# First tile and input block in pieces, and the first norm as row sums on ScalarE

## The reference, cut to what matters

```python
def rmsnorm(u, g):
    u32 = u.astype(jnp.float32)
    r = lax.rsqrt(jnp.mean(u32 * u32, axis=-1, keepdims=True) + NORM_EPS)
    return (u32 * r * g.astype(jnp.float32)).astype(u.dtype)
...
        h = rmsnorm(x, g[0])
...
    z = h @ w_in
    hy = dwconv3(z[..., :HY_STREAMS * D_HY], hy_short_w, hy_short_b)
```

## Time and profile before

| | before |
|---|---|
| median of three runs | 2406.3 us |
| profiled execution | 2411.59 us |
| its span, first to last instruction | 2409.7 us |
| mean granted TensorE clock | 0.993 |
| PE busy | 2368.3 us |
| DVE busy | 1327.8 us |
| ACT busy | 1096.8 us |
| DMA, mean | 185 GB/s |

### The profile page before, as it was taken

How to read it: one execution, slowest core, us unless ns; L and a number is a source line. 1 busy time by engine, 2 the same in 40 slices (tenths; PEclk the granted TensorE clock), 3 DMA queues, 4 the chain that set the end, 5 groups by cost and what they waited for, 6 DMA issues and landing times.

```text
span 2409.7 us, 25541 instructions
## 1 busy us (share of the span) xinstructions
PE 2368.3 (98%) x11089; PEld 1965.2 (82%) x11089; DVE 1327.8 (55%) x1318; ACT 1096.8 (46%) x1159; POOL 27.7 (1%) x49
## 2 busy tenths in 40 slices
PE   7999999999999999999999999999999999999998
PEld 6778787788888888888888888888888878888887
DVE  5565855544544554556764444554444576656554
ACT  5444443644443344344554444344344455544343
POOL 1000000000000000000000000000000000000000
PEclk9999999999999999999999999999999999999999
DMA  7445455555555555555455555555555545643344
GB/s 283 159 158 187 173 198 193 190 188 188 188 204 192 192 189 188 188 186 209 182 185 191 188 182 190 192 192 188 192 181 190 188 156 196 238 159 140 123 149 149
DMA packets 63103, 446.08 MB, mean 185 GB/s; under 512 B 7209, under 2 KB 7540, under 8 KB 11215
## 3 DMA queue, kind: packets, MB, share of 16 engines
q1 hardware_dynamic: 60080, 427.60, 49.8%
q0 software_dynamic: 2912, 16.85, 1.9%
HBM read 442.33 MB, written 2.10 MB: 184 GB/s over the span
## 4 chain that ended last, share of the span: by engine, by line
PE 92%; DVE 3%; DMA 2%; ACT 2%; issue 1%; POOL 0%; ACTq 0%; POOLq 0%; SPq 0%; DVEq 0%
PE P L329 89%; PE P L332 3%; DVE raw_r L596 1%; ACT hi L487 1%; DMA raw<-in_w_z 1%; DMA raw<-in_w_i 1%; DVE R_h L583 0%; DMA raw<-in_w_d 0%; DVE X L583 0%; DVE EV L639 0%; ACT R_h L483 0%; DVE R_m L580 0%; DMA raw<-in_w_u 0%; ACT EV L509 0%; DMA raw<-in_w_ukv 0%
## 5 line engine op out<-in xcount | busy, mean ns | idle before, releaser
L596 DVE TENSOR_TENSOR raw_r<-raw,hi 128x2048 fp32r<-128x2048 f32 (+3 forms) x412 | 928.3, 2256 | 955.5 <-ACT hi L487 955.1
L329 PE MATMUL P<-hi,R_h 128*128 128x512 f32 (+2 forms) x3840 | 1234.6, 396 | 17.9 <-DVE raw_r L596 10.9
L487 ACT ACTIVATE hi<-raw 128x2048 fp32r<-128x2048 f32 (+3 forms) x412 | 776.5, 1887 | 1010.8 <-DMA raw<-in_w_d 390.1
L329 PEld LDWEIGHTS P<-hi,R_h 128*128 128x128 f32 x3840 | 727.3, 190 | 170.2 <-DVE R_h L583 18.1
L329 PE MATMUL P<-hi,R_f_r 128*128 128x512 f32 x2480 | 777.3, 391 | 0.1
L329 PE MATMUL P<-raw_r,R_h 128*128 128x512 f32 (+2 forms) x1920 | 749.7, 390 | 0.0
L329 PEld LDWEIGHTS P<-hi,R_f_r 128*128 128x128 f32 x2480 | 465.6, 188 | 96.7 <-DVE raw_r L596 0.6
L329 PE MATMUL P<-raw_r,R_f_r 128*128 128x512 f32 x1240 | 482.7, 389 | 0.0
L329 PEld LDWEIGHTS P<-raw_r,R_h 128*128 128x128 f32 x1920 | 364.6, 190 | 73.7 <-issue 3.8
L329 PEld LDWEIGHTS P<-raw_r,R_f_r 128*128 128x128 f32 x1240 | 233.0, 188 | 47.1
L332 PE MATMUL P<-ident,EV 128*128 128x128 f32 (+2 forms) x486 | 72.5, 272 | 0.2 <-ACT EV L483 0.2
(11 more groups left out here) (192 smaller groups left out, 838.6 us busy)
## 6 DMA issues: line engine op xcount, KB each, us to landing
raw<-in_w_u SPq DMA_DIRECT2D x128, 1024.0 KB, 4.8
raw<-in_w_d SPq DMA_DIRECT2D x128, 1024.0 KB, 4.8
raw<-in_w_z SPq DMA_DIRECT2D x48, 1024.0 KB, 4.8
raw<-in_w_i SPq DMA_DIRECT2D x36, 1024.0 KB, 4.8
raw<-in_w_mo SPq DMA_DIRECT2D x16, 1024.0 KB, 4.8
raw<-in_w_o SPq DMA_DIRECT2D x16, 1024.0 KB, 4.7
raw<-in_w_mkv SPq DMA_DIRECT2D x8, 1024.0 KB, 4.8
R_g<-in_rows POOLq DMA_DIRECT2D x6, 1024.0 KB, 5.9
```

Source lines behind the costliest of these rows:

```text
L329: return self.e.matmul(o, l, r, start=start, stop=stop, skip_group_check=True)
L487: self.e.activation(hi, raw, ACT.Copy).then_inc(*self.inc("high_made", ("high", k, d)))
L596: self.e.tensor_tensor(low, raw, hi.bitcast(f32), ALU.subtract).then_inc(*self.inc("low_made", *names))
```

## The change

Four things are edited. First, tile 0 and the first of the four input blocks are loaded in pieces, each with a semaphore of its own, in turn: columns 0, slice 0, columns 1, slice 1, columns 2 and 3, slices 2 and 3; columns and splits of tile 0 alternate on ACT and DVE. Second, `cols` is loaded from ACT's queue, and ACT makes a first small copy (`first_table`) before the input is waited for, so that its table load stands there. Third, `X` is loaded from SP's queue behind `ident` and ahead of tile 4, in four pieces with a semaphore each; POOL's loads of the filter's tables wait for its last piece. Fourth, the first norm takes its sums from `X` with `square_sum` and the ordinary `rstd`; `first_squares` in its old form, `first_reduce` and `first_sums` are gone, and so is the wait of the bias load.

```diff
@@ -192,7 +192,6 @@
 
 
         self.XT = v3(R_g[:, :], 16)
-        self.SQ = R_m[:, :]
         self.f_emb, self.f_w1, self.f_w2 = R_s[0:33, 2048:2304], R_s[0:33, 2304:2368], R_s[0:64, 2368:2432]
         self.f_a, self.f_b = v3(R_f[:, 0:2048], 2), v3(R_f[:, 2048:4096], 2)
         self.f_win, self.f_w3 = v3(R_f[:, 4096:6144], 2), R_f[0:65, 6144:8192]
@@ -349,13 +348,6 @@
             last = self.tr(o, i)
         last.then_inc(*self.inc("turn_done", done))
 
-    def first_sums(self, b, src, ready, free, done):
-        self.wait_ge(free)
-        self.wait_ge(ready)
-        for t in range(2):
-            last = self.mm(self.m.P[b][:, t:t + 1], src[:, 128 * t:128 * t + 128], self.m.half[:, 0:1], True, True)
-        last.then_inc(*self.inc("turn_done", done))
-
     def filter_hidden(self, b, l, r, ready, free, done):
         self.wait_ge(ready)
         self.wait_ge(free)
@@ -483,7 +475,7 @@
         self.e.activation(o, i, ACT.Copy, **scale).then_inc(*self.inc("act_done", done))
 
     def split(self, k, d, hi, raw, low):
-        self.wait_ge(("loaded", k))
+        self.wait_ge(("loaded", k) if k else ("loaded", k, d))
         self.e.activation(hi, raw, ACT.Copy).then_inc(*self.inc("high_made", ("high", k, d)))
 
     def cols_ready(self, m):
@@ -498,10 +490,14 @@
         for d, g in enumerate(gains):
             self.copy(h[:, d, :], p[:, d, :], (done, "high", d), scale=g)
 
-    def first_squares(self, g, ready, done):
-        self.wait_ge(ready)
-        q = slice(1024 * g, 1024 * g + 1024)
-        self.e.activation(self.m.SQ[:, q], self.m.R_g[:, q], ACT.Square).then_inc(*self.inc("act_done", done))
+    def first_table(self, ready, done):
+
+        self.wait_ge(ready)
+        self.copy(self.m.st[:, 0:2], self.m.half[:, :], done)
+
+    def first_load(self, sem, o, i, done):
+        if sem == "c4":
+            self.e.dma_start(o, i).then_inc(*self.landed(sem, done))
 
     def square_sum(self, src, dst, o, ready, free, done, **scale):
         self.wait_ge(ready)
@@ -632,12 +628,6 @@
     def times_row(self, dst, src, row, ready, done):
         self.wait_ge(ready)
         self.tt(dst, src, row, ALU.mult, done)
-
-    def first_reduce(self, k, ready, free, done):
-        self.wait_ge(ready)
-        self.wait_ge(free)
-        self.e.tensor_reduce(self.m.EV[k][:, 0:256], self.m.SQ.rearrange("p (c t) -> p t c", c=16), AX.X, ALU.add
-                             ).then_inc(*self.inc("dve_done", done))
 
     def sine(self, z, cb, o, ready, done):
         m = self.m
@@ -920,8 +910,12 @@
         self.wait_ge(free)
         self.e.dma_start(o, i).then_inc(*self.landed(f"ring{k % NS}", ("loaded", k)))
 
+    def load_piece(self, d, o, i):
+        self.e.dma_start(o, i).then_inc(*self.landed(f"w{d}", ("loaded", 0, d)))
+
     def first_load(self, sem, o, i, done):
-        self.e.dma_start(o, i).then_inc(*self.landed(sem, done))
+        if sem != "c4":
+            self.e.dma_start(o, i).then_inc(*self.landed(sem, done))
 
     def store(self, t, q, ready, done):
         self.wait_ge(ready)
@@ -971,10 +965,7 @@
         while not listing and not at_["pause"] and at_["high"] < min(at_["load"], n):
             k = at_["high"]
             _, _, parts, c = plan[k]
-            n_ = 4 if k == 0 else 1
-            for d in range(n_):
-                q = slice(c // n_ * d, c // n_ * d + c // n_)
-                E.split(k, d, m.hi[k % NS][0:parts, q], m.raw[k % NS][0:parts, q], m.low[k % NS][0:parts, q])
+            E.split(k, 0, m.hi[k % NS][0:parts, 0:c], m.raw[k % NS][0:parts, 0:c], m.low[k % NS][0:parts, 0:c])
             at_["high"] += 1
 
     def take(name):
@@ -1269,56 +1260,65 @@
 
 
     XT, HH, HL, MH, ML, M, GA = m.XT, m.HH, m.HL, m.MH, m.ML, m.M, m.GA
-    id_m = mark("cols")
-    E.first_load("c4", m.cols[:, 0:a["cols"].shape[1]], a["cols"], id_m)
-    xt_m = []
+    id_m = [mark("cols"), mark("ident")]
+    E.first_load("c4", m.cols[:, 0:a["cols"].shape[1]], a["cols"], id_m[0])
+    half_m = mark("halves")
+    E.halves(half_m)
+    E.first_table(half_m, mark("table"))
+
+    def first_tile(d):
+        q = slice(512 * d, 512 * d + 512)
+        E.load_piece(d, m.raw[0][:, q], a["w_z"][0][:, q])
+
+    xt_m = [mark("xt") for _ in range(16)]
+    for c, n in ((0, 1), (1, 1), (2, 2)):
+        q = slice(256 * c, 256 * c + 256 * n)
+        for k in range(c, c + n):
+            xt_m[k] = xt_m[c]
+        E.first_load(f"xt{c}", m.R_g[:, q], a["xt"][0][:, q], xt_m[c])
+        for d in range(c, c + n):
+            first_tile(d)
+    at_["load"] = 0 if listing else 1
+    for g in range(1, 4):
+        for k in range(4 * g, 4 * g + 4):
+            xt_m[k] = xt_m[4 * g]
+        E.first_load(f"c{g}", m.R_g[:, 1024 * g:1024 * g + 1024], a["xt"][g], xt_m[4 * g])
+        load_ahead(g + 1)
+    E.first_load("c14", m.ident[:, :], a["c_ident"], id_m[1])
+    x_m = [mark("x") for _ in range(4)]
     for g in range(4):
-        xt_m.append(mark("xt"))
-        E.first_load(f"c{g}", m.R_g[:, 1024 * g:1024 * g + 1024], a["xt"][g], xt_m[g])
-        load_ahead(g + 1)
-    id_m = [id_m, mark("ident")]
-    E.first_load("c14", m.ident[:, :], a["c_ident"], id_m[1])
+        E.first_load(f"x{g}", m.X[:, :, 512 * g:512 * g + 512], a["x"][g], x_m[g])
     side_load("c5", m.f_emb, a["c_emb"])
     side_load("c5", m.f_w1, a["w_f1"])
     f_m = side_load("c5", m.f_w2, a["w_f2"])
-    half_m = mark("halves")
-    E.halves(half_m)
     E.cols_ready(id_m[0])
 
     h_m, r1_m, sq_m = [None] * 16, [], []
 
-    def first_columns(g):
+    def first_column(c):
+        in_columns(XT[:, c, :], xt_m[c], HH, HL, GA[0], c, h_m)
+
+    def first_squares(g):
+        sq_m.extend(square_sum(m.piece(t, g), m.SUMB[:, t, g:g + 1], x_m[g]) for t in range(2))
+
+    def first_norm():
+        first_squares(3)
+        r1_m.append(rstd(m.SUMB, D, m.R1, list(sq_m)))
+
+    for c in range(4):
+        first_column(c)
+        q = slice(512 * c, 512 * c + 512)
+        E.split(0, c, m.hi[0][:, q], m.raw[0][:, q], m.low[0][:, q])
+    at_["high"] = 0 if listing else 1
+    for g in range(1, 4):
         for c in range(4 * g, 4 * g + 4):
-            in_columns(XT[:, c, :], xt_m[g], HH, HL, GA[0], c, h_m)
-
-    def first_squares(g):
-        sq_m.append(mark("squares"))
-        E.first_squares(g, xt_m[g], sq_m[g])
-
-    def first_reduce():
-        k, done = ev(hold=True), mark("reduced")
-        E.first_reduce(k, list(sq_m), ev_free[k], done)
-        sq_m.append(done)
-        sq_m.append(k)
-
-    def first_sums():
-        k = sq_m.pop()
-        b, done = bank(), mark("sums")
-        E.first_sums(b, EV[k], [list(sq_m), half_m, id_m], bank_free[b], done)
-        let_go(k, done)
-        r1_m.append(rstd(P[b][:, 0:2].rearrange("p (t g) -> p t g", t=2), -D / 2, m.R1, done))
-        bank_free[b] = list(r1_m)
-
-    for g in range(4):
-        first_columns(g)
+            first_column(c)
         if g < 3:
             split_ahead(g + 1)
-    later += [lambda g=g: first_squares(g) for g in range(4)] + [first_reduce, nop, nop, nop, nop, first_sums]
-    side_load("c6", m.f_w3, a["w_f3"], xt_m[3])
+    later += [nop] * 5 + [lambda g=g: first_squares(g) for g in range(3)] + [first_norm]
+    side_load("c6", m.f_w3, a["w_f3"], x_m[3])
     side_load("c6", m.f_win.rearrange("p t n -> p (t n)"), a["c_win"])
     f3_m = side_load("c6", m.R_s[:, 0:1024], a["c_dft"])
-    for g in range(4):
-        x_m = side_load("c15", m.X[:, :, 512 * g:512 * g + 512], a["x"][g], f3_m)
 
     fl = {}
 
@@ -1368,7 +1368,7 @@
         k_names.append(half_dft(which, src[:, :, g], dst[:, 0, g], dst[:, 1, g], fl["m"]))
 
     def load_bias():
-        fl["b"] = side_load("c16", m.brow, a["hy_bias"], list(sq_m))
+        fl["b"] = side_load("c16", m.brow, a["hy_bias"])
 
     extra += [load_bias, filter_1, nop, nop, nop, filter_2, nop, nop, nop]
     extra += [lambda t=t, g=g: filter_3(t, g) for g in range(4) for t in range(2)]
```

More of the change, by code:

```diff
@@ L317 @@
         cmp_values_out = cols_ready = compress = copy_out = copy_turned = double = filter_hidden = filter_out = \
-        filter_sums = final_row = final_scale = finish = first_load = first_reduce = first_squares = first_sums = gate = \
-        gated_silu = gated_v = gates = half_dft = half_silu = halved_rstd = halves = head_columns = inverse = load_tile = \
+        filter_sums = final_row = final_scale = finish = first_load = first_table = gate = \
+        gated_silu = gated_v = gates = half_dft = half_silu = halved_rstd = halves = head_columns = inverse = load_piece = load_tile = \
         masked_exp = memory_out = mla_out = nsa_out = ones_row = plain_exp = plain_parts = padded_keys = pool_scale = pool_windows = \
@@ L2153 @@
 SEMAPHORES = (["product_done", "turn_done", "high_made", "act_done", "low_made", "dve_done", "pow_done", "row0", "row1", "stored"]
-              + [f"ring{k}" for k in range(NS)] + [f"c{k}" for k in range(17)])
```

(1 more changed line is left out.)

## The result

The changed kernel takes 2410.75 us (median of 17 runs, 2405.3 to 2416.1), the kernel before 2406.94 in the runs beside them (17, 2401.7 to 2408.8). The ratio is 1.0017, 95% interval 1.001 to 1.0023: slower by 3.8 us, where 8.2 us less were forecast, and outside the range given. The profiled execution of the change took 2410.8 us.

A forecast was written before the change was run, and what follows sets the result against it. PE, busy 2368.3 of 2409.7 us, was taken as the bound. Start 2.1, reduce wait 6.5 and low clock 2.6, less a new wait of 3.0, gave 8.2 us off 2406.3: 2398.1 us, 8-in-10 range 2394.5 to 2404.5.

The forecast's parts named there:

- Start: First tiles: PE starts at 5.8 us and reaches tile 1 at 16.1 instead of 18.2, a gain of 2.1 us.
- The bytes ahead of tile 1 are the same, and it landed at 2.60 + 9.1 = 11.7: Start of SP's queue: tile 1 still lands at 11.7 us despite the pieces, so PE can reach it at 16.1.
- Nothing of it is lost below 0 unless tile 1 lands after 13.8: Start: the gain of 2.1 us may shrink, but turns into a loss only if tile 1 lands after 13.8 us.
- Rival (e): Start: the pieces delay tile 1 past 13.8 us, 2 us are missing, the rest holds: 2400 us; chance 0.05.
- PE between tile 1 and the transposes: Tiles 1 to 4 and half of tile 5 run without other waits, from 16.1 to 40.4 us.
- If it keeps its place, it lands at 29.4: Tile 5, queued behind tile 4 and before POOL's loads, lands at 29.4 us if it keeps that place.
- Rival (a): Fair sharing from POOL's first byte holds up tile 5 until 34.5 us: gain 3.1 us, 2403 us; chance 0.2.
- rival (b): Tile 6 lands late, at 37.5 to 38.5 us, and the clock falls: gain 3.4 to 6.4, about 2401.5; chance 0.2.
- The norm: First norm: the reduce's wait goes; the first transposes come 7.8 us after tile 6's split can start, at 43.4 us.
- I reckon with no fall of the clock in it: PE's new 3.0 us wait before the first transposes lowers no clock; a fall would lose 1.5 to 2.5 us.
- The sum: Up to the first transposes: 2.1 + 6.5 + 2.6 − 3.0 = 8.2 us gained, or 0.34%.
- Behind 57 us: Behind the first transposes every engine has the same work in the same order, with PE nearly always busy.

The follow-up runs named there:

- Start_only: The kernel before with only the changed start (pieces, cols on ACT's queue, early table load) and the old norm: 2408.32 us, ratio 1.0005.
- half_pieces: The changed kernel with four transfers instead of seven for the first block and tile 0: 2407.24 us, ratio 1.0003.
- mid_pieces: The changed kernel with the start of before (whole transfers) and tile 2 loaded in four column slices: 2407.91 us, one run.
- norm_only: The changed kernel with the start of before, so the new norm and load order alone: 2407.12 us, ratio 1.000 to before.
- late_tables: The changed kernel with POOL's three loads of the filter's tables waiting for tile 6 instead of x: 2403.71 us, ratio 0.9985 to before.
- before_again: The kernel before, unchanged, run again as a control and for a second profile: 2408.64 us, ratio 1.001 to before.

## Why the prediction was wrong

**Start: the step that failed was "The bytes ahead of tile 1 are the same, and it landed at 2.60 + 9.1 = 11.7".** The bytes were, but for cols, the rate wasn't: 14.3. PE started at 6.95 (5.8 predicted) and came to tile 1 at 18.68 (16.1), behind a wait of 3.69 us (1.9) with a fall of the clock, which the prediction didn't have at all. "Nothing of it is lost below 0 unless tile 1 lands after 13.8" named the right condition; it was met, and the effect on all later landings wasn't priced. Rival (e) has this mechanism, with 5 in 100 and without that effect. Start_only shows the late tile 1 alone, half_pieces and mid_pieces its size.

**PE between tile 1 and the transposes.** 24.3 us predicted (16.1 to 40.4), 26.1 measured: 1.8 for the lower clock behind the wait at tile 1.

**Landings: "If it keeps its place, it lands at 29.4".** It didn't keep its place. Tile 5 came at 35.48: 3.1 us because tile 4 came at 30.03, not 26.9 (2.8 of it the start's, since norm_only had tile 4 at 27.22), and 2.95 for the tables (T, shown by late_tables). Rival (a), with 2 in 10, had this mechanism and 34.5. The row on which I chose against it (30.5 to 33.5) was x from POOL's queue against a tile, 0.06 MB against 1.01; in the change POOL's tables (w_f3, 0.53 MB, and the head of c_win) against a tile went the other way, 0.94 against 0.22 MB. The section of the Trainium skill that the prediction names beside rival (a) ("DMA: Bandwidth & Descriptors", "Queues, rings and completion order") speaks of turns, a packet at a time; neither row shows even shares (14 packets against 140, 143 against 42).

Tile 6 came at 42.26, not at 35.6, past the last value of rival (b) too. It was issued at 31.22 instead of 26.9, since PE was late with tile 2, and took 11.0 us instead of 8.7; with late tables it took 4.8. By the prediction's own chain and its 2 us for the clock, the change loses from a landing of about 41.9 on (51.7 - 7.8 - 2), and none of its rivals goes there. (Its gain for rival (b), 3.4 to 6.4, forgets these 2 us at the upper end, which is 4.4.)

**The norm.** The chain from the last split on was right: 7.75 us from 42.26 to 50.01, 7.8 predicted. The reduce's wait is gone, as predicted; its cost of 9.1 us was read from one execution, and in before_again it is 8.5. But the wait that took its place was 5.2 us, not 3.0, and **"I reckon with no fall of the clock in it"** failed as well: 4.93 us for twelve products, 2.2 more than at full clock. Even the 3.0 us that were forecast were not safe from it: the earlier trace rows has a fall behind 2.9 idle us in 4, and in start_only one followed a wait of 2.55 us.

**The sum.** Predicted 8.2 gained by the second transposes. Measured against the same execution of before: 2.6 lost at tile 1, 1.8 in the pace, 2.2 in the wait and 2.6 behind it (5.85 us from the first transposes to the second, 3.2 before), 9.2 together: 1.0 us lost, and the transposes say the same (55.86 against 54.89). Against the other execution of before it is 2.0 (53.90).

**Behind 57 us** the prediction had the same work at the same pace. It is the same work, but not always at the same pace. The issue times of the weight tiles in SP's timeline show where. Against before_again the change lies about 2 us back up to 413 us, 1.1 from 441 on, 3.2 from 1227 on, 4.3 from 2084 on and 4.4 at the end. It moves in steps at a few places, and so does the first profile of before against before_again (1.1 to 1.3, then 1.5, 3.5 and 5.1). Norm_only, 1.4 us ahead up to 413 us, ends 3.7 us back, and 3.9 us of that come in two steps between 2046 and 2069 us. In 2060 to 2072 us its clock fell (0.86), where start_only, which has the old norm and the same work there, kept 1.00:

```profile
2060.00:2072.00 12.00, 10.52 (x49) 8.46 (x48) 6.60 (x4) 7.56 (x8) 0.58 (x1) 0.86 0.76 282
```
```profile
2060.00:2072.00 12.00, 11.18 (x69) 9.35 (x68) 6.57 (x4) 7.60 (x8) 0.58 (x1) 1.00 0.80 282
```

So of the 3.8 us that the change costs, 1.0 to 2.0 are placed in the first 57 us. The rest is of the size of such steps, which the same kernel has too from one execution to another; that they are its cause in the median is argued, not shown, and it stays open.

## What to carry to other kernels

Pieces at the head of a queue start the first product sooner and make everything behind them later; what counts is when the second tile comes, so count transfers as well as bytes. Two edits that each cost nothing clear alone can cost together, when one makes the time hang on what the other delays. When a load is released by another, ask which tiles are then in the queue: here the tables, which by the prediction's reckoning nothing reads before 59 us, took the engines from the two tiles that stood before the norm. And work on an in-order engine whose data is there belongs ahead of a split that waits for a transfer; a wait removed from PE is only gained if nothing behind it has a wait of the same length in store.

## What the runs showed of the hardware

- Transfers of 128 to 256 KB at the start of the program cost a little under 0.5 us each in the landings behind them (two, four and seven transfers for the same 1.5 MB), with the DMA engines at 101%, 98% and 86% of their time in 2 to 9 us; in the middle of a full queue 0.2 to 0.3 us.
- Four transfers onto 32 partitions each moved 1.71 MB in 7 us with the engines at 95% of their time, where transfers onto 128 partitions moved 2.54. POOL's queue, with w_f3 onto 65 partitions and behind it the head of c_win onto 128, held 85.5% of the engines' time for 0.94 MB in 5 us, about half the rate per busy time of a tile (1.01 MB in 3 us for 84.2%).
- PE's wait and the clock behind it (before tile 1, at the reduce, at the transposes): no fall after 0.7, 0.9 and 1.7 us; a fall after 2.5 (start_only's reduce) and 3.7, with some 1.8 us lost in the second; and ten and eleven of the next twelve products at 1.2 GHz after 4.9 (norm_only) and 5.2 (the change). A wait of 1.90 us that ended at 1220.49 in start_only and at 1220.38 in before_again was followed by a fall in start_only (0.72 in 1221 to 1227) and by none in before_again (1.00):

```profile
1221.00:1227.00 6.00, 6.00 (x25) 4.87 (x25) 4.09 (x7) 5.10 (x9) 0.00 (x0) 0.72 0.29 123
```
```profile
1221.00:1227.00 6.00, 6.00 (x33) 5.01 (x32) 4.08 (x7) 6.00 (x10) 0.00 (x0) 1.00 0.26 109
```

The same short wait, 0.1 us sooner or later, thus came with a fall in one kernel and with none in the other; in the change it ended at 1222.01, with a fall (0.72 again).
